# A two-layer transformer kernel in one core: operand splits two slabs ahead, paired evacuations, norm sums moved into the output projections

## The reference

```python
# layer 1 (w_in: 2048 x 4608, 8 query heads, 2 kv heads of 128, pooling branch)
h = rmsnorm(x, pre_g) * (1 + scale) + shift          # shift, scale, gate = silu(c) @ w_ada + b_ada
q, k, v, gate_a, u, gate_p = split(h @ w_in)
y_a = windowed_gqa(q, k, v, rel_table, sink) * silu(gate_a)
y_p = multiscale_pool(u, w_pool_grp, pool_scale) * silu(gate_p)
g_a, g_p = split(sigmoid(h @ w_merge + b_merge))
o = (g_a * (y_a @ w_br_attn) + g_p * (y_p @ w_br_pool)) @ w_out
x = x + gate * rmsnorm(o, post_g)
# layer 2: mixer (16 query heads of 64 in a window, rope; gated linear attention, 4 heads), then a conv FFN
sh1, sc1, g1, sh2, sc2, g2 = split(silu(c_2) @ w_mod + b_mod)
h = rms(x, mix_pre) * (1 + sc1) + sh1
y = (sigmoid(g_a) * (attn(h) @ w_br_a) + sigmoid(g_b) * (gla(h) @ w_br_b)) @ w_out
x = x + g1 * rms(y, mix_post)
h = rms(x, ffn_pre) * (1 + sc2) + sh2
y = (silu(conv3(gate_part)) * conv3(value_part)) @ w_down     # gate, value = split(h @ w_up), 2 x 5632
x = x + g2 * rms(y, ffn_post)
```

## Time and profile before

| what | value |
|---|---|
| median of 3 runs | 2522.36 us |
| profiled execution, own time | 2521.72 us |
| its span, first to last instruction | 2519.9 us |
| PE busy | 2312.4 us (92%) |
| DVE busy | 1789.0 us (71%) |
| ACT busy | 1153.7 us (46%) |
| mean granted TensorE clock | 0.951 |

### The profile page before, as it was taken

The page is one execution under the profiler, slowest core; times in us unless marked ns, Lnnn a source line. Parts: engine busy times, 40 slices in busy tenths (PEclk is TensorE's granted clock), DMA queues, the critical chain, the costliest instruction groups (busy, mean ns, idle before and its releaser), DMA issues.

```text
span 2519.9 us, 32064 instructions
## 1 busy us (share of the span) xinstructions
PE 2312.4 (92%) x12836; PEld 1982.0 (79%) x12836; DVE 1789.0 (71%) x2282; ACT 1153.7 (46%) x1637; POOL 94.1 (4%) x113
## 2 busy tenths in 40 slices
PE   2499999999995889999999999997999999989997
PEld 1388888888784768888888888886888888878886
DVE  6767777779854787777677888646777777764444
ACT  1343455555445345454455455445444444434443
POOL 1000000000000000000011100000000000000000
PEclk8599999999996989999999999998999999999998
DMA  9867778878843757578777788743555555556662
GB/s 380 353 229 271 260 260 286 292 269 308 307 158 120 258 175 259 202 248 293 263 262 256 253 291 306 268 167 117 186 198 184 171 197 184 189 158 188 188 184 80
DMA packets 313032, 580.67 MB, mean 230 GB/s; under 512 B 12187, under 2 KB 105167, under 8 KB 308533
## 3 DMA queue, kind: packets, MB, share of 16 engines
q1 hardware_dynamic: 300224, 535.86, 62.3%
q0 software_dynamic: 11328, 40.26, 4.9%
q10 hardware_dynamic: 1332, 2.51, 0.3%
HBM read 557.61 MB, written 20.97 MB: 230 GB/s over the span
## 4 chain that ended last, share of the span: by engine, by line
PE 60%; DVE 9%; ACT 4%; issue 2%; DMA 0%; DVEq 0%; ACTq 0%
PE gemm L1607 38%; PE gemm L1608 19%; DVE w_lo L985 2%; DVE mod_acc L978 1%; PE extra L1430 1%; ACT w_hi L676 1%; ACT quad_work L676 1%; PE extra L1422 1%; DVE proj L1057 1%; ACT scores L676 0%; ACT operand_main L676 0%; DVE small L1198 0%; DVE scores L1195 0%; DVE proj L1054 0%; PE extra L1516 0%
## 5 line engine op out<-in xcount | busy, mean ns | idle before, releaser
L1607 PE MATMUL gemm<-operand_main,w_hi 128*128 128x512 f32 x4880 | 1740.0, 404 | 72.9 <-issue 26.5
L1608 PE MATMUL gemm<-operand_main,w_lo 128*128 128x256 f32 x4880 | 1329.3, 283 | 0.0
L1607 PEld LDWEIGHTS gemm<-operand_main,w_hi 128*128 128x128 f32 x4880 | 911.9, 191 | 281.0 <-issue 44.3
L985 DVE TENSOR_TENSOR w_lo<-w_stage,w_hi 128x1024 fp32r<-128x1024 f32 (+2 forms) x774 | 876.0, 1160 | 361.1 <-ACT w_hi L676 360.6
L676 ACT ACTIVATE w_hi<-w_stage 128x1024 fp32r<-128x1024 f32 (+2 forms) x776 | 766.3, 1007 | 653.5 <-PE gemm L1608 652.4
L1608 PEld LDWEIGHTS gemm<-operand_main,w_lo 128*128 128x128 f32 x4880 | 934.7, 192 | 30.1
L978 DVE SCALAR_TENSOR_TENSOR mod_acc<-mod_stage,c_silu,mod_acc 128x1024 f32<-128x1024 f32 x224 | 285.4, 1315 | 0.6 <-DMA mod_stage<-in_w_mod 0.6
L676 ACT ACTIVATE low_part<-gemm 128x256 f32<-128x256 f32 x329 | 125.4, 384 | 326.7 <-PE gemm L1607 302.6
L1607 PE MATMUL gemm<-ffn_hidden,w_hi 128*128 128x512 f32 x704 | 249.8, 401 | 9.8 <-issue 9.8
L1608 PE MATMUL gemm<-ffn_hidden,w_lo 128*128 128x256 f32 x704 | 196.1, 282 | 0.0
L1607 PEld LDWEIGHTS gemm<-ffn_hidden,w_hi 128*128 128x128 f32 x704 | 132.5, 190 | 41.7 <-issue 10.1
(11 more groups left out here) (198 smaller groups left out, 1214.5 us busy)
## 6 DMA issues: line engine op xcount, KB each, us to landing
w_stage<-in_w_in SPq DMA_DIRECT2D x128, 1024.0 KB, 6.2
mod_stage<-in_w_mod SPq DMA_DIRECT2D x192, 512.0 KB, 5.6
w_stage<-in_w_up SPq DMA_DIRECT2D x88, 1024.0 KB, 5.0
w_stage<-in_w_down SPq DMA_DIRECT2D x64, 704.0 KB, 4.8
w_stage<-in_w_ada SPq DMA_DIRECT2D x32, 1024.0 KB, 8.0
w_stage<-in_w_merge SPq DMA_DIRECT2D x32, 1024.0 KB, 5.5
w_stage<-in_w_out SPq DMA_DIRECT2D x32, 1024.0 KB, 5.5
mod_stage<-in_w_ada SPq DMA_DIRECT2D x32, 512.0 KB, 6.0
```

The lines of the kernel that those rows point to most:

```text
L985: tt(WL[:, s1 % 2, c0:c1], WST[:, s1 % 4, c0:c1], WH[:, s1 % 2, c0:c1].bitcast(F32), ALU.subtract)\
L1607: hi = lambda **kw: mm(bank[:, :], WH[:, s % 2, c0:c0 + P], X_[:, k, :], **kw)
L1608: lo = lambda **kw: mm(bank[:, T:2 * T], WL[:, s % 2, c0:c0 + P], X_[:, k, 0:T], **kw)
```

## The change

Much more than the norm stages is rewritten. What changes, part by part:

1. Weights: the ring has 5 slots and the low part is made in place, so a slot is free only when TensorE has used the slab. `w_hi` has three buffers. Splits run two slabs ahead (s+2); they start when slab s-1 is used whole.
2. Evacuation goes by pairs of tiles: ScalarE copies the low halves of two banks straight to the destination, VectorE adds the high halves in one instruction of 512 elements. The next group's first bank waits for the whole first pair.
3. out1, out2 and down: the squares and sums of the quarters already finished run as hook `out_sq` behind slab 2 of the next phase; ScalarE also scales the output by gate x norm weight there. `mod_end` 4 and 8 move into out1 and out2. After the last slab only half quarters are left. VectorE alone makes the new residual, a multiplication and an addition of whole quarters.
4. `prep_h` goes by tiles of 256 elements (two VectorE instructions and one ScalarE instruction each), and the first group multiplies tile by tile.
5. The last norm's sums are per token (one column); the residual and the output's first three quarters are transposed in hooks behind down's slabs; VectorE's last step is done on token rows.
6. Convolution without the padded copy; the last block is finished behind down's first slabs; down's groups are four tiles wide with 11 slabs of 4 chunks.
7. In qkvb `attn5` of the first pair is a hook of slab 3, so it stands before the group's evacuation. branch1 carries 3 modulation rows per phase (before 2, the rest in out1), branch2 4 rows per 6 slabs (before 6 per 12).
8. SyncE holds the fifth modulation row's load until the small vectors and x have landed.

```diff
+RAW, HIS, AHEAD = 5, 3, 2
+        WST = at("w_stage", [P, RAW, SLAB], F32, o_wst)
+        WL = at("w_lo", [P, RAW, SLAB], F32R, o_wst)
+        WH = at("w_hi", [P, HIS, SLAB], F32R, take(HIS * 8 * KB))
...
+            phases.append(Phase("branch1", i, [Group(A["w_branch_attn"][0], 512 * i, 2, "attn", "merge_a", n=i),
+                                               Group(A["w_branch_pool"][0], 512 * i, 2, "main", "merge_b", n=i)],
+                                mod=(4, 3 * i, 3), pre=[] if i else [("poolmix", 0), ("prep_y", 1)]))
+        for i in range(4):
+            phases.append(Phase("out1", i, [Group(A["w_out"][0], 512 * i, 4, "main", "proj", tile=16 + 4 * i)],
+                                hooks={2: [("out_sq", (0, i - 1))]} if i else {}, mod=(4, 12 + 2 * i, 2) if i < 2 else None,
+                                pre=[] if i else [("prep_merged", 0)], post=([], [("mod_end", 4)], [], [("resid", 0)])[i]))
...
+            phases.append(Phase("qkvb", i, [two(1536 + 1024 * i, 12 + 8 * i), two(2048 + 1024 * i, 16 + 8 * i)],
+                                hooks={**attn(0, pair[0]), **attn(4, pair[1]), 3: [("attn4", pair[0]), ("attn5", pair[0])]},
+                                late=[("attn5", pair[1])],
+                                mod=((5, 6, 5), (5, 11, 5), (6, 0, 4), (6, 4, 4))[i], post=[("mod_end", 5)] if i == 1 else []))
...
+            phases.append(Phase("branch2", i, [Group(A["w_branch_attn_2"][0], 512 * i, 2, "attn", "merge_a", n=4 + i),
+                                               Group(A["w_branch_gla_2"][0], 512 * i, 4, "main", "merge_b", n=4 + i)],
+                                mod=(8, 4 * i, 4), pre=[] if i else [("prep_y", 2)]))
...
+                behind = {0: [("ffn_val", 10)], 1: [("ffn_hi", 10)], 2: [("ffn_lo", 10)], **{4 + c: [("x_turn", c)] for c in range(4)}}
+            else:
+                behind = {2: [("out_sq", (2, i - 1))], 4: [("o_turn", i - 1)]}
+            phases.append(Phase("down", i, [Group(A["w_down_2"][0], 512 * i, 11, "hid", "late", tile=4 * i)], hooks=behind,
...
@@ ScalarE @@
+            def split_hi(n):
+                for h, c0, c1 in halves(n):
+                    if h == 0:
+                        act.wait_ge(w_landed[slot_of(n)], landed(n))
+                    if h == 0:
+                        positive(act, slab_used, n - HIS + 1)
+                    activate(WH[:, n % HIS, c0:c1], WST[:, slot_of(n), c0:c1], ACT.Copy).then_inc(hi_made, 1)
...
@@ VectorE, resid of the two mixers @@
+                    norm_rs(norm_of[("resid", k)])
+                    dve.wait_ge(start["resid_in"], 16 * (k + 1))
+                    dve.wait_ge(o_scaled, 5 * k + 5)
+                    for js in ((0, 1), (2, 3)):
+                        for j in js:
+                            o = PROJ[:, 16 + 4 * j:20 + 4 * j, :]
+                            ins = tt(o, o, RSQ, ALU.mult)
+                        link(ins)
+                        for j in js:
+                            x = PROJ[:, 32 + 4 * j:36 + 4 * j, :]
+                            tt(x, x, PROJ[:, 16 + 4 * j:20 + 4 * j, :], ALU.add).then_inc(new_x, 1)
...
@@ VectorE, prep_h by tiles @@
+                            stt(WORK[:, s % 8, :], src[:, src0 + s, :], AFF[:, s:s + 1], RS[:, :], ALU.mult, ALU.mult).then_inc(scaled, 1)
...
+                            stt(HL[:, t, T:2 * T], WORK[:, t % 8, :], MODV[:, shift + t:shift + t + 1], HL[:, t, 0:T].bitcast(F32),
+                                ALU.add, ALU.subtract).then_inc(op_ready, 1)
...
@@ VectorE, the loop over slabs @@
+                for s, (g, q) in enumerate(ph.slabs):
+                    if ph.slab0 + s + AHEAD < len(slabs):
+                        split_lo(ph.slab0 + s + AHEAD)
+                    for h in ph.hooks.get(s, ()):
+                        hook(*h)
+                    for r in mods_behind(ph, s):
+                        mod_row(ph, r)
+                    if q == g.slabs - 1:
+                        evac(g)
+                for h in ph.late:
+                    hook(*h)
...
@@ TensorE @@
+            def gemm(n):
...
+                for m, kc in order:
+                    k = q * QUAD + kc
+                    if k == 0 and m % 2 == 0 and g.gi:
+                        before = groups[g.gi - 1]
+                        wait_evac(pe, before, min(m // 2 + 1, before.pairs))
+                    if by_tile and m == 0:
+                        pe.wait_ge(op_ready, op_count[name] - 16 + k + 1)
...
@@ SyncE @@
+                if t == 4:
+                    sp.wait_ge(start["vec_in"], 16 * sum(len(p) for p in packs[1:]))
+                    sp.wait_ge(start["x_in"], 16)
```

More of the change, by code:

```diff
@@ L223, in build @@
         w_in2 = A["w_in_2"][0]
[L226 to L231 removed]
+        phases = []
+        one = lambda c: Group(w_in, c, 4, "main", "proj", tile=c // P)
@@ L236, in build @@
-        segs[-1].groups[0].kw["tile_step"] = 12
-        segs.append(Segment("gate_p1", 1, [gp(4096)], mod=(2, 2, 14), post=[("mod_end", 2), ("silu1", 0), ("v1", 0)]))
-        for kv in range(2):
-            arg = dict(blk=1, kv=kv, first=4 * kv)
-            segs.append(Segment(f"merge{kv}", 4, [Group(w_merge, 2048 * kv, 512, 4, "main", "gate", bias=col["b_merge"] + 16 * kv,
-                                                        slot=16 * kv)],
-                                hooks=attn_hooks(0, arg), late=attn_late(0, arg), mod=(3, 2, 8 * kv), post=[("mod_end", 3)] if kv else []))
@@ L277, in build @@
[L277 to L292 removed]
+        for i in range(2):
+            phases.append(Phase("in_gates", i, [one(2048 + 1536 * i)], mod=(2, 10 + 2 * i, 2)))
@@ new lines, in build @@
+        n_pairs, mods = 0, 0
+        for ph in phases:
+            ph.slab0 = len(slabs)
+            ph.mod0 = mods
+            mods += 2 * ph.mod[2] if ph.mod else 0
+            for g in ph.groups:
+                g.gi = len(groups)
+                groups.append(g)
+                g.pair0, g.full0 = n_pairs, n_pairs - g.gi
+                n_pairs += g.pairs
+            for s, (g, q) in enumerate(ph.slabs):
+                g.last = len(slabs)
+                slabs.append((ph, g, q))
@@ L293, in build @@
+        named = lambda name: [ph for ph in phases if ph.name == name]
+        first = lambda name: named(name)[0]
         MOD0_ROWS = 32
@@ new lines, in _ @@
+                if ph.name in ("out1", "out2", "down") and i == 0:
+                    load_resid({"out1": 0, "out2": 1, "down": 2}[ph.name])
+                if ph.name == "merge":
+                    pool.wait_ge(start["lines_stored"], 16 * HEADS1)
+                    positive(pool, biased, i)
+                    for b in range(2):
+                        at0 = 255 - P * b
+                        pool.dma_start(BIAS[:, b, :], lines[i, at0:at0 + P * (LINE - 1)].rearrange("(q k) -> q k", k=LINE - 1)[:, 0:T])\
+                            .then_inc(bias_landed, 16)
+                    store_gate(0, ph.groups[0])
@@ L659, in _ @@
+                for what, k in ph.post:
                     stage(what, k)
@@ L901, in _ @@
[L901 to L913 removed]
+            groups_up = [g for g in groups if g.evac == "ffn"]
@@ L1325, in _ @@
[L1325 to L1334 removed]
+            ups = [g for g in groups if g.evac == "ffn"]
@@ L1369, in _ @@
+                for h in ph.late:
+                    hook(*h)
+                for what, k in ph.post:
+                    stage(what, k, ph)
         @block.tensor
```

1190 lines of the change are left out of this document (555 added, 635 removed).

## The result

| kernel | median, us | range | ratio to before, 95% interval |
|---|---|---|---|
| before | 2523.04 | 2521.14 to 2526.69 | |
| after | 2554.49 | 2549.60 to 2556.48 | 1.0120 (1.0101 to 1.0139) |

The kernel became 31.5 us slower; 15.6 were forecast. The profiled execution after has an own time of 2549.6 us (span 2547.6), the lowest of its four, 27.9 more than the one before (2521.7).

What follows compares the result with a forecast made beforehand. PE was taken as busy 92% of the span, leaving 207 us idle and what busy time hides. From 2521.7, wins of 41 and costs of 3, 14.3, 8.5, 6, 15.5 and 10 gave 2538 us; range 2503 to 2566.

Steps and rivals of the forecast that it cites:

- (a): Behind out1 and out2: gap of 21.8 us in place of 39.1, 9.6 moved between slabs; 15.4 won in all.
- (b): Waits for low parts in qkv2 and first slabs of branch2 and up: 7.8 us won by splitting ahead.
- (c): Before down: the 9.8 us wait goes, and about 2 of slow clock behind it; 11.8 us won.
- (d): Tail 13.2 us against 30.7, with 11.4 us of transposes and sums added in down: net 6.1 won.
- (e): Head: norm operand by tiles starts TensorE later, and the fifth row's load is held; 3 us lost together.
- (f): qkvb slab 3: `attn5` before the evacuation costs 4.7 us in two phases, 2.45 in two: 14.3 lost.
- (g): Splits starting later delay in-loop chains: 8.5 us lost in qkvb's attention units, 6 in gates2.
- (h): branch1 and branch2: a modulation row at slab 1 stalls each of 8 phases by 2.5 us; 15.5 lost.
- (i): Clock falls behind a few new stalls and the moved `mod_end`: 10 us lost, for six of them.
- rival B: Slower still: the clock falls behind all 24 new stalls, 40 us in place of 10; 2568 us, chance 0.13.
- A: Faster: the extra split buffer lets VectorE's evacuation at group ends mostly arrive in time; 2494 us, chance 0.27.
- D: Behind out1 and out2 the chain takes as long as the moved work saves, (a) at 0: 2554 us.

Runs made afterwards that it cites:

- e2: Changed kernel with `attn5` of qkvb's first pair moved behind the evacuation of slab 3, on ScalarE and VectorE: 2534.10 us.
- e6: Kernel of e4 with the modulation rows placed as in the kernel before the change: 2508.69 us.
- e7: Kernel before the change with only the new placement of the modulation rows: 2553.97 us.
- e4: Changed kernel with `mod_end` moved behind the residual step of the last phase of out1 and out2: 2542.73 us.
- e5: Changed kernel with splits one slab ahead in place of two, rings and orders kept: 2581.08 us.
- e11: Best kernel until then (2485.61 us) with VectorE's split behind hook and evacuation at the last slab of each gates2 group: 2472.37 us.

## Why the prediction was right and wrong

The direction and the mechanism were right: slower, because evacuations come late at group ends. The size was half of what came. By the prediction's letters, forecast against measured in the profiled executions (with -1.5 in other stretches the measured terms add up to 27.9; the forecast ones make 16.3):

| term | forecast | measured | from |
|---|---|---|---|
| (a) norms behind out1, out2 | -15.4 | -7.8 | windows, pair starts |
| (b) low parts | -7.8 | -9.6 | qkv2, up's first block, branch2's first slab |
| (c) before down, clock behind it | -11.8 | -12.1 | windows, pair starts |
| (d) tail and down | -6.1 | -17.8 + 9.3 = -8.5 | |
| (e) head | +3 | +0.9 | |
| (f), (g) in qkvb | +22.8 | +17.3 of stall | pair starts; e2 for (f) |
| (g) in gates2 | +6 | +4.2 | pair starts |
| (h) branches | +15.5 | +30.0 of stall | pair starts; e6, e7 |
| (i) clock | +10 | +10.9 in the branches, +4.1 in qkvb | |

**The step that failed is (h)**, "2.5 us of stall in each of 8 phases; before, some 0.5 in branch1", hence 15.5. It measured 30.0: 29.2 behind slab 1, 3.7 a phase, where no stall stood before, and 0.8 at the last phases' ends. With the clock, and less the 2.2 us of (b) at branch2's first slab, the branch phases are 38.7 us longer than before; moving the rows back wins 34.0 (e6). e7 shows the rows alone: the old kernel with nothing but their new placement takes 2554.0 us, as much as the changed kernel. The mechanism and the order of VectorE's work stood as it came, in the phase shown above: a phase's slabs end 11.3 us from its start, as forecast, and the row before is through at 7.6 (forecast 7.45). But the load of row 1 was timed from 6.3, when row 0's first half is used. The half that counts is the second, whose load can begin only at 7.6; it took 5.1, so the row ended at 14.1 in place of 13.1, the addition at 14.7 in place of 13.8, and TensorE went on at 14.8. The late load is 1.0 us here, of the 1.2 a phase by which 2.5 was short. The rest is in the middle value: eight times 2.5 are 20, and 15.5 took off what the branches were said to lose before and more, without a row for it. The upper bound of 30 is what came, and its condition ("landing 5.6 throughout") is near the DMA issues of branch2 after:

```profile
mod_stage<-in_w_mod SPq DMA_DIRECT2D x30, 512.0 KB, 5.8
```

**(i)** was six stalls at 1.65 and fell short next. The slow matmuls grew in every branch phase and in all of qkvb's: 15.0 in branches and qkvb and 4.5 more in out1 and out2 (counted in (a)), less 2.0 in up and 0.8 in qkv2. The rival B had this mechanism and its 24 stalls at 1.65, 40 us; about half of it came. That the sum missed by no more than 11.6 us is luck: (a), (h) and (i) together came out 27 us worse than forecast, and everything else 15 us better.

**(a)** is half its size, the third term that failed. The gap is 24.9, not 21.8, and the moved work costs more in the stream than its own time. Timeline behind out1 after:

```profile
774.87 0.47 ACT L645 ACTIVATE rstd<-extra,small 128x256 f32<-128x256 f32 x1 [0.28 <-PE extra L1407]
775.38 1.75 DVE L982 RECIPROCAL rstd<-rstd 128x256 f32<-128x256 f32 x1 [2.98 <-ACT rstd L645]
777.16 2.36 DVE L1044 TENSOR_TENSOR proj<-proj,rstd 128x1024 f32<-128x1024 f32 x2
...
785.87 1.06 ACT L645 ACTIVATE quad_work<-proj 128x1024 f32<-128x1024 f32 x1 [2.86 <-PE extra L1407]
...
788.02 1.06 ACT L645 ACTIVATE quad_work<-proj 128x1024 f32<-128x1024 f32 x1 [1.09 <-PE extra L1407]
...
791.92 1.75 DVE L982 RECIPROCAL rstd<-rstd 128x256 f32<-128x256 f32 x1 [5.33 <-ACT rstd L645]
```

The eight instructions of VectorE alone took 9.4, with 9.6 forecast (777.16 to 786.6). The last square did not start there but at 788.02: it waited for one of two work buffers, which TensorE's sums, at a granted clock of 0.73 (782.5 to 790), had not yet read. That and the first squares, which ScalarE interleaves with the scaling, are the 3.1. In the stream `mod_end` lost 2.4 of clock behind it besides its own 4 (e4).

**(f)** was right to 0.1 us a phase: 4.7 and 2.45 were forecast (its own addends make 5.9 with the row, not 5.7); the gaps behind slab 3 went from 1.3 to 5.9, 5.9, 3.7 and 3.7, which is 4.6 and 2.4. e2 gives it back, and 6.0 of clock with it. **(g)** had the right place and too much of it in qkvb: the waits behind slabs 2 and 6 grew by 3.1 us together where 8.5 were forecast (eight by 1.1 are 8.8); one slab ahead wins 12.4 there (e5). In gates2 13 us hang on where the split stands (e11), not on how early it is issued. **(b)** holds: slab 2 of qkv2 waits 7.5 us where 7 were forecast. **(c)** holds with its 2 us of clock: the first eight pairs of down lost 2.4 us before, at a granted clock of 0.78 over 12.2 us, and the first 13.8 us of down now have 1.00. **(d)** was right in its parts. A group of transposes lengthens the stream by 0.87 (forecast 0.85) and a group of one-column sums by 1.79 (half of 3.63); down is 9.3 us above full clock in all, forecast 11.4, and the tail 17.8 shorter, forecast 17.5. **(e)** can't be told from one profiled execution each: the first GEMM matmul starts at 130.6 to 135.7 in kernels that don't differ there. The 32 instructions of its norm took 12.8 us, as the row gave it.

Of the rivals, A (the evacuations arrive in time) is excluded by the waits and C by the time. D named 2554, the time that came, but that is a coincidence: the gaps behind out1 and out2 did shrink, by 14.4 each, and (a) won 7.8. Of the signs of being wrong, one came: stalls larger than in (h).

## What to carry to other kernels

On an in-order engine, nothing that can wait, and nothing long, belongs in front of the instruction that frees the accumulation banks; work with two slabs of slack goes behind it. An attention part and a split put there were worth 23 and 13 us of 2554. The rows were worth 18.6 put there and 34 placed where no group ends, since behind neighbouring slabs they make a stall elsewhere. Where the long instruction also waits for a load, time that load from the release of its own buffer, at the landing time of a busy stretch, and add to each stall half of the slow stretch behind it. Filler work deserves a timing by itself: here its placement cost as much as the whole change seemed to.
